# Wider gate_up loads, a second conditioning part summed on the vector engine, and a reordered front in a one-core decoder layer

## The reference, cut to what matters

```python
mod = (c @ w_ada + b_ada)                    # 6 x 1024: sh1, sc1, gt1, sh2, sc2, gt2
h = rms_norm(x, g_norm1) * (1 + sc1) + sh1
dn_qkv, z, b, a, fx_qkv, f, gate_a, gate_b = split(h @ w_in)
o_a = gated_delta_rule(...)                  # chunks of 64, from silu(conv(dn_qkv))
o_a = rms_norm(o_a, g_onorm) * silu(z);  y_a = o_a @ w_o_delta
y_b = forgetting_attention(fx_qkv, f) @ w_o_fox
x = x + gt1 * ((sigmoid(gate_a) * y_a + sigmoid(gate_b) * y_b) @ w_out)
h2 = rms_norm(x, g_norm2) * (1 + sc2) + sh2
# top 4 of 32 experts, per expert:
gu = h2[tokens] @ w_gate_up[e] + b_gate_up[e]     # 1024 x 2048, 8 MiB
act = (clip(up) + 1) * gate * sigmoid(1.702 * gate)
y += weight * (act @ w_down[e] + b_down[e])       # 1024 x 1024, 4 MiB
out = rms_norm(x + gt2 * y, g_final)
```

## Time and profile before

| | before |
|---|---|
| median of 3 runs | 1228.27 us (1225.92 to 1231.68) |
| the profiled execution's own time | 1225.72 us, its span 1223.9 us |
| PE busy | 1130.1 us (92%) |
| DVE / ACT / POOL busy | 337.1 / 185.5 / 108.8 us |
| bytes moved | 464.71 MB, mean 380 GB/s |

### The profile page before, as it was taken

The page is one execution under the profiler, slowest core; times in us unless marked ns, Lnnn a source line. Parts: engine busy times, 40 slices in busy tenths (PEclk is TensorE's granted clock), DMA queues, the critical chain, the costliest instruction groups (busy, mean ns, idle before and its releaser), DMA issues.

```text
span 1223.9 us, 15032 instructions
## 1 busy us (share of the span) xinstructions
PE 1130.1 (92%) x6251; PEld 582.7 (48%) x6251; DVE 337.1 (28%) x682; ACT 185.5 (15%) x317; POOL 108.8 (9%) x50
## 2 busy tenths in 40 slices
PE   5999999999999999988989889999999999989886
PEld 2999799878433434433333333333433433333322
DVE  1633557341422121321221212122122312212102
ACT  2465344001200000100000000000001000000002
POOL 0764444020000000000000000000000000000000
PEclk9999999999999999999999999999999999999999
DMA  9973765498999999999999999999999999999995
GB/s 352 340 224 103 241 238 207 132 369 333 418 421 428 427 428 428 428 428 428 428 428 428 428 428 428 428 428 428 428 429 428 428 428 428 428 428 428 428 427 245
DMA packets 62559, 464.71 MB, mean 380 GB/s; under 512 B 8469, under 2 KB 31130, under 8 KB 34618
## 3 DMA queue, kind: packets, MB, share of 16 engines
q1 hardware_dynamic: 61688, 462.92, 92.0%
q10 hardware_dynamic: 786, 1.14, 0.3%
q0 software_dynamic: 48, 0.13, 0.0%
HBM read 463.13 MB, written 1.05 MB: 379 GB/s over the span
## 4 chain that ended last, share of the span: by engine, by line
PE 68%; DMA 24%; issue 2%; DVE 2%; ACT 2%; SPq 0%; POOL 0%; DVEq 0%; ACTq 0%
PE ps L506 65%; DMA ring<-in_w_down_dram 12%; DMA ring<-in_w_gate_up_dram 6%; DMA kept<-in_w_down_dram 4%; DMA ring<-in_w_ada_dram 2%; PE ps L973 1%; ACT kept L1324 1%; POOL w_lo L1846 0%; PE ps L1005 0%; ACT w_hi L1130 0%; SPq L350 0%; DVE ring L1537 0%; DVE ring L1531 0%; PE ps L533 0%; DVE kept L1406 0%
## 5 line engine op out<-in xcount | busy, mean ns | idle before, releaser
L506 PE MATMUL ps<-ring,kept 128*64 128x512 f32 (+2 forms) x2984 | 651.3, 599 | 34.8 <-DMA ring<-in_w_down_dram 17.7
L506 PEld LDWEIGHTS ps<-ring,kept 128*64 128x64 f32 (+2 forms) x2984 | 210.5, 138 | 449.5 <-issue 397.0
L506 PE MATMUL ps<-kept 128*128 128x128 f32 (+4 forms) x984 | 192.2, 408 | 8.3 <-ACT kept L1324 3.3
L506 PEld LDWEIGHTS ps<-kept 128*128 128x128 f32 (+2 forms) x984 | 108.3, 176 | 94.5 <-issue 81.8
L1320 ACT ACTIVATE kept<-kept 128x512 f32<-128x512 f32 x32 | 20.2, 630 | 727.7 <-DVE kept L1748 727.7
L1748 DVE TENSOR_SCALAR kept<-ps 128x512 f32<-128x512 f32 x32 | 22.1, 692 | 385.9 <-PE ps L506 385.9
L1770 DVE TENSOR_TENSOR kept<-ps,kept 64x512 f32<-64x512 f32 x64 | 44.1, 689 | 293.8 <-PE ps L506 292.8
L1846 POOL TENSOR_TENSOR w_lo<-ring,w_hi 128x1024 fp32r<-128x1024 f32 x38 | 94.6, 2508 | 107.4 <-ACT w_hi L1130 107.4
L506 PE MATMUL ps<-hT_hi,w_hi 128*128 128x256 f32 x272 | 78.5, 289 | 0.4 <-POOL w_lo L1846 0.4
L506 PE MATMUL ps<-hT_lo,w_hi 128*128 128x256 f32 x272 | 76.9, 283 | 0.0
L506 PE MATMUL ps<-hT_hi,w_lo 128*128 128x256 f32 x272 | 76.8, 282 | 0.0
(11 more groups left out here) (231 smaller groups left out, 536.5 us busy)
## 6 DMA issues: line engine op xcount, KB each, us to landing
ring<-in_w_gate_up_dram SPq DMA_DIRECT2D x127, 2048.0 KB, 27.6
ring<-in_w_down_dram SPq DMA_DIRECT2D x47, 2048.0 KB, 23.5
kept<-in_w_down_dram SPq DMA_DIRECT2D x16, 2048.0 KB, 24.5
ring<-in_w_ada_dram SPq DMA_DIRECT2D x24, 1024.0 KB, 7.1
ring<-in_w_in_dram SPq DMA_DIRECT2D x22, 1024.0 KB, 10.1
ring<-in_w_out_dram SPq DMA_DIRECT2D x4, 1024.0 KB, 13.7
ring<-in_w_o_fox_dram SPq DMA_DIRECT2D x2, 1024.0 KB, 6.3
ring<-in_w_o_delta_dram SPq DMA_DIRECT2D x2, 1024.0 KB, 7.7
```

What stands on the lines that cost most here:

```text
L506: return pe.matmul(dst, lhsT, rhs, start=start, stop=stop, skip_group_check=True)
```

## The change

There are four edits.

1. **gate_up rows by four.** Partition p now holds rows 4p to 4p+3 of 512, so that a load of 4 tiles (4 MiB) has 32 KiB contiguous in each partition. In the pairs between the first and the last one gate_up load is 4 MiB (`load_gu(e, par, v)`), issued when all four tiles are free, and PE waits for it once in four tiles. The first fills and the last pair stay in halves of 2 MiB (now two pieces of 16 KiB with a pitch of 32 KiB); the first reload is 1 MiB and then 3 MiB. The permutation of `h2tok`, the router rows and the conditioning columns follow (`run_rows`, `run_vecs`, `runs_of`).
2. **Part 1 of the conditioning is summed on the vector engine** (`SUMMED = (1, 2)`), its blocks stand earlier in `UNITS`, between the `fqk` blocks, and `add_rows(1, k)` stands after the convolutions 3 to 5 (k = 0 to 2) and after `rowF_taken` (k = 3 to 7). `ada(1, 5)` on PE becomes `ada_over_rows(1, 5)` ahead of `z`.
3. **The pair products stand between the two z projections** instead of behind both.
4. **`take_yb(0)`**, the vector engine's product on the first fox group, stands ahead of the last chunk's step.

```diff
-        UNITS += win_part("fqk", COL_FOX, range(4)) + win_part("fv", COL_FOX + 2 * W, (0, 1))
-        UNITS += win_part("z", COL_Z, (0, 1)) + ada_part(1)
+        UNITS += ada_part(1, (0, 1)) + win_part("fqk", COL_FOX, (0, 1)) + ada_part(1, (2, 3))
+        UNITS += win_part("fqk", COL_FOX, (2,)) + ada_part(1, (4,)) + win_part("fqk", COL_FOX, (3,))
+        UNITS += ada_part(1, (5, 6, 7)) + win_part("fv", COL_FOX + 2 * W, (0, 1)) + win_part("z", COL_Z, (0, 1))
...
-        SUMMED = (2,)
+        SUMMED = (1, 2)
...
-            def load_gu(e, par, u):
-
-                src = w_gate_up[0, e, u * 2 * P:(u + 1) * 2 * P, :].rearrange("(p k) n -> p (k n)", k=2)
-                s0 = par * KD + 2 * u
-                sp.dma_start(flat[:, s0 * UNIT:(s0 + 2) * UNIT], src).then_inc(expert_chunk_sem(s0), 16)
...
+            def gu_rows(e, v):
+                return w_gate_up[0, e, v * 4 * P:(v + 1) * 4 * P, :].rearrange("(p k) n -> p k n", k=4)
+
+            def load_gu(e, par, v, k0=0, kk=4):
+
+                s0 = par * KD + 4 * v + k0
+                sp.dma_start(flat[:, s0 * UNIT:(s0 + kk) * UNIT].rearrange("p (k n) -> p k n", k=kk),
+                             gu_rows(e, v)[:, k0:k0 + kk, :]).then_inc(
+                    expert_chunk_sem(s0 if kk == 2 else par * KD + 4 * v), 16)
...
-            def next_gu(I, i, par, us=range(4)):
-
-                for u in us:
-                    sp.wait_ge(S("gu_used"), I * 16 + (par * KD - 16 + 2 * u + 2))
-                    load_gu(i * 2 + par, par, u)
+            def next_gu(I, i, par, vs=range(2)):
+
+                for v in vs:
+                    sp.wait_ge(S("gu_used"), I * 16 + (par * KD - 16 + 4 * v + 4))
+                    load_gu(i * 2 + par, par, v)
...
-                        for k in range(2):
-                            sp.wait_ge(S("gu_used"), I * 16 + (k - 15))
-                            load_gu_row(i * 2, 0, 0, k)
+                        for k0, kk in ((0, 1), (1, 3)):
+                            sp.wait_ge(S("gu_used"), I * 16 + (k0 + kk - 16))
+                            load_gu(i * 2, 0, 0, k0, kk)
...
-                for i, late in zip(range(TURN, PAIRS - 1), (4, 3, 2, 1, 0, 0)):
+                for i, late in zip(range(TURN, PAIRS - 1), (2, 2, 1, 1, 0, 0)):
...
+            ada_over_rows(1, 5)
             project("z", 0)
-            project("z", 1)
             pe.wait_ge(S("tok_taken"), 1)
             chunk_pairs((2, 7), kn, kn).then_inc(S("pairs_ps"), 1)
...
             chunk_pairs((3, 4), kn, qn).then_inc(S("pairs_ps"), 1)
-            pe.wait_ge(S("rowF_taken"), 1)
-            ada(1, 5)
+            project("z", 1)
             mod_transposes(1, 6)
...
-                    if k % 2 == 0:
+                    if k % 4 == 0:
                         pe.wait_ge(expert_chunk_sem(par * KD + k),
...
                 last.then_inc(S("conv_ready"), 1)
+                if u >= 3:
+                    add_rows(1, u - 3)
...
             last.then_inc(S("rowF_taken"), 1)
+            for k in range(3, KD):
+                add_rows(1, k)
...
             last.then_inc(S("tok_taken"), 1)
+            take_mod_rows(1, 5)
             dve.wait_ge(S("pairs_ps"), 1)
...
             TTn(qn, qn, exg, ALU.mult).then_inc(S("qd_ready"), 1)
-            take_mod_rows(1, 5)
             take_mod(1, 6)
...
                     if n < 2:
                         add_rows(2, 5 + 2 * n)
+                    else:
+                        take_yb(0)
...
             take_mod_rows(2, 6)
-            take_yb(0)
             take_yb(1)
```

More of the change, by code:

```diff
@@ L143, in layer_kernel @@
         x1sq = keep(3072, 1024).rearrange("p (t n) -> p t n", t=TT)
-        run_rows = keep(8448, 256)
+        run_rows = keep(o + 2793, 512)
         mod_rows = keep(8704, 512)
@@ L403, in _ @@
             sp.wait_ge(S("yb_ps"), 4)
-            load_gu(0, 0, 3)
-            load_gu(1, 1, 2)
+            load_gu(0, 0, 1, 2, 2)
+            load_gu(1, 1, 1, 0, 2)
             sp.wait_ge(S("ya_ps"), 4)
-            load_gu(0, 0, 0)
-            load_gu(1, 1, 3)
+            load_gu(0, 0, 0, 0, 2)
+            load_gu(1, 1, 1, 2, 2)
             sp.wait_ge(S("merged_ready"), 4)
-            for u in range(2):
-                load_gu(1, 1, u)
+            for half in range(2):
+                load_gu(1, 1, 0, 2 * half, 2)
             sp.wait_ge(S("out_ps"), 4)
-            for u in (1, 2):
-                load_gu(0, 0, u)
+            load_gu(0, 0, 0, 2, 2)
+            load_gu(0, 0, 1, 0, 2)
             sp.wait_ge(S("gt2_ps"), 1)
@@ L439, in high_of_last @@
                         next_dn(I, i, 0, 1)
-                for u in range(4):
-                    if u == late:
+                for v in range(2):
+                    if v == late:
                         high_of_last()
-                    if u == 0 and not first_unit_whole:
-                        for k in range(2):
-                            sp.wait_ge(S("gu_used"), I * 16 + (k - 15))
-                            load_gu_row(i * 2, 0, 0, k)
-                    else:
-                        next_gu(I, i, par, range(u, u + 1))
-                if late == 4:
+                    if v == 0 and not first_unit_whole:
+                        for k0, kk in ((0, 1), (1, 3)):
+                            sp.wait_ge(S("gu_used"), I * 16 + (k0 + kk - 16))
+                            load_gu(i * 2, 0, 0, k0, kk)
+                    else:
+                        next_gu(I, i, par, range(v, v + 1))
+                if late == 2:
                     high_of_last()
                 next_dn(I, i, par, 0)
-                if late == 5:
+                if late == 3:
                     high_of_last()
@@ L529, in mod_transposes @@
                     pe.wait_ge(S("run_in"), 64)
-                    for k in range(2):
-                        pe.transpose(bank(5, 256 + 16 * k, 12), run_rows[0:12, k:256:2], ident[0:12, 0:12])
+                    for k in range(4):
+                        pe.transpose(bank(5, 256 + 16 * k, 6), run_rows[0:6, k:512:4], ident[0:6, 0:6])
                 for s in range(4):
@@ L535, in mod_transposes @@
                     rows = slice(64, P) if part == 1 else slice(0, 64)
-                    runs = mod_rows.rearrange("p (u n k) -> p u k n", u=2, k=2)
+                    runs = mod_rows.rearrange("p (n k) -> p k n", k=4)
                     for j in range(4):
-                        last = pe.transpose(bank(5, j * 64, 64), runs[rows, j // 2, j % 2, :], ident[rows, rows])
+                        last = pe.transpose(bank(5, j * 64, 64), runs[rows, j, :], ident[rows, rows])
                 last.then_inc(S("mod_cols_ps"), 1)
@@ L951, in gate_up_bias, with gate_up @@
                     mm(bank(4 + b), sel_r[:, par, :], bias_r[:, b, :], True, False)
-            def gate_up(i, par, first=False, opening=False):
+            def gate_up(i, par, first=False, opening=False, halves_before=None):
                 extra = 16 if par == 0 and not opening else 0
@@ L1031, in pair @@
             def pair(i, high, first, opening=False):
-                gate_up(i, 0, first, opening)
+                gate_up(i, 0, first, opening, 0 if opening else None)
                 if opening:
@@ L1042, in pair @@
                 scat_transposes()
-                gate_up(i, 1)
+                gate_up(i, 1, halves_before=0 if opening else None)
                 pe.wait_ge(S("y_moved"), i * 4 + 2)
@@ L1053, in last_pair @@
             def last_pair(i, high, q):
-                gate_up(i, 0)
+                gate_up(i, 0, halves_before=q + 1)
                 pe.wait_ge(S("y_moved"), i * 4)
@@ L1059, in last_pair @@
                 gate_up_bias(i, 1)
-                gate_up(i, 1)
+                gate_up(i, 1, halves_before=q + 1)
                 pe.wait_ge(S("act_t_ready"), i * 2 + 1)
@@ L1592, in _, with take_yb @@
                         S("fox_p_ready"), 1)
+            def take_yb(g):
+                dve.wait_ge(S("yb_ps"), g + 1)
+                gb_ms = gates[:, 8 + 2 * g:10 + 2 * g, :]
+                TTn(gb_ms, bank(g % 2).rearrange("p (m n) -> p m n", m=2), gb_ms, ALU.mult).then_inc(S("yb_taken"), 1)
             add_rows(2, 3)
```

44 lines of the change are left out of this document (21 added, 23 removed).

## The result

| | before | after |
|---|---|---|
| median of the timed runs (20 each), us | 1228.41 | 1231.32 |
| ratio of after to before, 95% interval | | 1.0022 [1.0012, 1.0031] |
| profiled execution: its own time, its span, us | 1225.7, 1223.9 | 1229.1, 1226.8 |
| mean granted clock | 0.986 | 0.979 |

The change makes the kernel 2.9 us slower (1228.41 x 0.0022 = 2.7; the interval is 1.5 to 3.8). The forecast was 0.9 us faster (1227.4 against the 1228.3 shown with the profile).

What follows compares the result with a forecast made beforehand. DMA bytes over rate bound it from about 345 us on, mostly PE's chain before. From 1225.7 us, +3.6 - 1.5 + 1.0 - 4.0 = -0.9 gave 1224.8, as a median 1227; 8-in-10 range 1217 to 1236.

Steps and rivals of the forecast that it cites:

- The likeliest case: The main forecast: a stop of PE at fv 0, 431 GB/s in the middle, median 1227 us; chance 0.48.
- Part 1: From v's transposes to gates 0, PE saves most conditioning blocks and a wait: 5.8 us gained.
- Part 2: At fv 0, issued late behind additions, PE stops; v's transposes 9.4 us late, +3.6 net of the gain behind fv.
- far bound: Latest end of POOL's split of fv 0, both halves behind all additions: 119.9 us.
- The clock's part: Behind PE's stop at fv 0, work at half clock: about 1.7 us lost.
- Part 3: Ahead of the third fox group, the wait for `take_yb` goes: 1.5 us gained, or 0.
- Part 4: gate_up loads by 4 MiB: +1.0 us at the first pair, nothing in the middle's queue, -4.0 us from the rate.
- the gap of the first pair: At the first gate_up reloads near 322 us, DMA loses 1.6 us and closes 0.7: +1.0, at most 2.5.
- The middle: Between first and last pairs, later loads and longer PE waits cost nothing against a 22.7 us queue.
- The wider rows bring nothing: Rival: 32 KiB rows in gate_up loads give no rate gain, all else as forecast; median 1231 us, chance 0.18.
- No stop: Rival: in the front PE doesn't stop at fv, which gains 5.8 + 1.5 us; median 1218 us, chance 0.22.
- Slower rows: Rival: wider gate_up rows run at 422 GB/s, +7.8 us; median 1239 us, chance 0.12.

Runs made afterwards that it cites:

- c3: Kernel after plus 30 useless 128x256 products on PE ahead of fv 0, filling part of its stop: 1230.70 us, ratio 1.0016 to the kernel before.
- b4: Kernel before with only the first fox group's product (take_yb) taken sooner: 1228.72 us, ratio 1.0000.
- b2: Kernel after with ACT's four b_gate_up loads issued ahead of the last take of the fox projections: 1228.86 us, ratio 1.0004 to the kernel before.
- a1: Kernel after with additions 3 to 7 of part 1 moved into the vector engine's earlier pauses: 1228.42 us, ratio 0.9992 to the kernel before.
- a3: Kernel after with all gate_up loads at 2 MiB (first reload 1, 1, 2), leaving the front alone: 1234.46 us, ratio 1.0051 to the kernel before.
- a4: a1 with the first pair's gate_up reloads in pieces of 1 and 2 MiB as before the change: 1227.27 us, ratio 0.9991 to the kernel before.
- b1: Kernel after with addition 3 early, 4 and 5 behind the running sums' copy, 6 and 7 unmoved: 1218.80 us, ratio 0.9927 to the kernel before.
- c1: Kernel after with only addition 3 of part 1 moved to the pause behind the gates' small columns: 1223.44 us, ratio 0.9964 to the kernel before.
- a2: Kernel before with the 4 MiB gate_up loads alone: 1226.26 us, ratio 0.9983.
- c4: Kernel after with the edits of b1 and b2, a4's first-pair pieces, and all gate_up loads at 2 MiB or less: 1221.96 us, ratio 0.9940 to the kernel before.

## Why the prediction was wrong

The likeliest case was the right one, with its stop and its rate, and it was off by 3.8 us (2.9 slower against 0.9 faster). By its steps:

- **Part 1**, PE's gain behind fv: 5.8 forecast. From v's transposes to gates 0 it is 25.2 us before (123.48 to 148.73) and 20.1 in the kernel after (134.73 to 154.84): 5.1. The mechanism is the forecast's, down to the wait for the split of gates 0 (1.37 us, 1.6 forecast), and the size is right within 0.7.
- **Part 2**, the late fv 0: 9.4 forecast for v's transposes, 9.95 measured from the first convolution (80.5 against 70.55). PE had fv 0 at 119.7 (120.96 with the start's 1.3 us taken off) where I took 118.5. I had the mechanism and chose the middle of its range instead of working it through. Turn by turn my own numbers give the measured end: the fourth addition ends at 103.33 + 4 x 2.35 = 112.7, a half follows to 115.1, the last addition to 117.5, the other half to 119.9. My far bound was also 119.9, but for another reason (both halves behind all the additions, 115.1 + 4.76), so that the bound held was luck. The clock's part was near (1.2 us by c3 against 1.7). Together with part 1 +4.8 where +3.6 stood, inside the bounds of +2.3 and +6.7.
- **Part 3 is the step that failed**: "Gain 1.5 us; if the last step's new values come late in return, 0." The wait did go, but b4 shows 0.0 for this edit alone (-1.4 to +1.5), and b2 shows that in the changed kernel the meeting behind it costs 2.2 to 2.5 us, so that by my estimate the edit made it up to 1 us slower (-1.5 + 2.5). I had looked at whom the product waits for, and not at what the steps behind it would run into 1.6 us sooner. The meeting is the usual case: eight profiled executions have the product at its new place and the bias loads at their old one, and in seven (a1, a3, a4, b1, b4, c1, c3) the step takes 1.55 to 2.37 us; the kernel after's own is the one that got through. Taken together the two steps miss by 1.2 + 2.5 = 3.7 of the 3.8 us. This sum is an estimate: the first term is from two profiled executions, the second has the noise of two medians.
- **Part 4**: the gap of the first pair is there. From 322 to 338 us 16 x (1 - 341/430) = 3.3 us of transfers are missing and 4 x (1 - 395/430) = 0.3 from 338 to 342, against 0.7 before: 2.9 more. Less of it reaches the end. The two profiled spans differ by 2.9 us, of which 1.3 lie ahead of the first convolution, 4.8 ahead of gates 0, -1.6 from there to the first down loads (99.9 against 101.5) and 1.4 from there to the first reload (62.3 against 60.9). That leaves -3.0 for all of part 4, its forecast to the tenth: +1.0 and -4.0. a2, at -2.1, agrees. The middle costs nothing (the DMA share is 1.00 from 345 us on), and 32 KiB packets last 1218 ns in the median against 614 for 16 KiB, 10 ns less for the same bytes, where I had derived 9 from shorter ones.
- **The rivals.** "The wider rows bring nothing" had the right number, 1231, for a wrong reason: a2, a3 and c4 exclude it. "No stop" is what b1 makes of the kernel, 1218.8 for its 1218. "Slower rows" is excluded.

The Trainium skill, "SBUF — State Buffer", section "Who interferes with whom", which I had used for POOL's side alone, covers the vector engine's too: a vector instruction "with two SBUF inputs contends with a GpSimd instruction that reads SBUF", and whoever comes second blocks for the whole of the other instruction, whatever its own size. The runs agree: 2.37 us for 16 elements in a1, 2.34 for 8 in b4. By the section a step with at most one input in SBUF doesn't contend, and the kernel before shows that too. In its timeline L1390, with one input in PSUM, runs in 0.18 us beside a bias split that lasts from 251.08 to 253.44; L1630, with both in SBUF, ends at 253.48, just behind the split:

```profile
251.08 2.36 POOL L1857 TENSOR_TENSOR bias_r<-kept,bias_hi 32x1024 fp32r<-32x1024 f32 x1
...
252.88 0.18 DVE L1390 TENSOR_TENSOR kept<-ps,kept 128x16 f32<-128x16 f32 x1 [4.28 <-PE ps L538]
...
253.17 0.31 DVE L1630 SCALAR_TENSOR_TENSOR kept<-kept 128x8 f32<-128x8 f32 x1
```

The kernel before also has a step that is held up, ahead of the running sums: L1468, 16 elements, takes 1.78 us and ends when POOL's split does (87.49 + 4.73 = 92.22), and PE waits 2.07 us behind it.

```profile
87.49 4.73 POOL L1846 TENSOR_TENSOR w_lo<-ring,w_hi 128x1024 fp32r<-128x1024 f32 x2 [5.16 <-ACT w_hi L1130]
...
90.47 1.78 DVE L1468 TENSOR_TENSOR kept<-kept 128x16 f32<-128x16 f32 x1 [2.88 <-ACT kept L1188]
```

This is the short stop at 92 us of the earlier trace rows. I took the clock's fall from it and didn't ask what made the stop. The answer was the mechanism that part 3 lacks.

Open: all profiled executions but three (the kernel before, a1 and c1) have a stretch of the clock at 0.5 that begins between 302 and 320 us, where PE waits up to 1.3 us at a time. In the kernel after it makes 32 products last 5.21 us instead of 3.81, the 1.4 us above. Whether the kernel before has it in most of its runs too, its one profile can't say; a2 and b4, whose programs have the same order there, both have it (from 312.0 and 313.2 us on). In how many of its executions the kernel after meets the bias split isn't shown either.

## What to carry to other kernels

An edit that makes one engine's chain earlier moves all its later steps too: before counting the gain, lay the chain at its new times beside POOL's two-input operations, and look for vector steps with both inputs in SBUF, however small. A load that waits for a slow chain of additions needs only the one addition that frees its tile, so put that one into a pause and leave the rest. And where two engines exclude each other, don't take the middle of a range: let them take turns, one whole instruction each, and add up.

## What the runs showed of the chip

- The vector engine and POOL, both with two inputs in SBUF, take turns by whole instructions: an addition of 2.35 us lasts 4.25, a POOL half of 2.4 us 4.39. Small steps pay as much as large ones: four of 8 to 16 elements took 9.2 us in a1.
- Whether they meet is decided by some tenths of a microsecond: 0.13 us ahead of the split, 0.15 us long; 0.02 us behind it, 2.37.
- PE waited 2.1 to 2.5 us for that step in six profiled executions, and in five of them (a1, a3, b4, c1, c3; not a4) the clock's record went to 0.5 for 3.4 us there; in the other eight the wait was 0.3 to 1.7 us, and it didn't.
- A row of 32 KiB is one packet on this chip (6476 of them from 400 to 1150 us in the kernel after) and takes 0.8% less than two of 16 KiB (1218 against 2 x 614 ns).
